# Gated delta rule in a fused two-block kernel: per-token norm factors in place of normalised keys and queries, and split gate rows spread in one pass

## What is computed

```
q = l2norm(q) * 128**-0.5 ; k = l2norm(k)          # per token and key head
g = -exp(a_log) * softplus(a + dt_bias) ; gc = cumsum(g)   # per chunk and value head
decay[i, j] = exp(gc[i] - gc[j]) for i >= j, else 0
L = strict_lower((k * beta) k^T * decay)
u, w = solve(I + L, [v * beta, k * beta * exp(gc)])
o = (q * exp(gc)) S + (q k^T * decay)(u - w S)      # S: the state of the chunk before
o = o * rsqrt(mean(o*o) + 1e-6) * norm_w * silu(z)
```

## Time and profile before

| what | before |
|---|---|
| median of 3 runs | 2850.68 us (2849.74 to 2850.77) |
| profiled execution: span, first to last instruction | 2847.0 us |
| PE, PEld, DVE, ACT, POOL busy | 96%, 84%, 68%, 42%, 29% |
| mean granted PE clock | 0.986 |
| the 8 iterations of the delta rule | about 170 to 975 us |
| one steady iteration | 98.86 us |

### The profile page before, as it was taken

How to read it: one execution, slowest core, us unless ns; L and a number is a source line. 1 busy time by engine, 2 the same in 40 slices (tenths; PEclk the granted TensorE clock), 3 DMA queues, 4 the chain that set the end, 5 groups by cost and what they waited for, 6 DMA issues and landing times.

```text
span 2847.0 us, 51314 instructions
## 1 busy us (share of the span) xinstructions
PE 2720.7 (96%) x20214; PEld 2404.2 (84%) x20214; DVE 1949.3 (68%) x2285; ACT 1208.2 (42%) x1521; POOL 812.5 (29%) x554
## 2 busy tenths in 40 slices
PE   6999999999997999999999999969999999999998
PEld 4788988898895777888888888769899999999996
DVE  1377877787778677666666666676999898555554
ACT  2255455545544444333333333344333334433343
POOL 1066666666667510000000000001555552000000
PEclk8999999999999999999999999989999999999999
DMA  9866666676665666666665555535554555555554
GB/s 364 311 195 214 223 216 200 205 247 199 200 223 169 212 184 207 187 191 189 188 188 187 189 189 186 167 115 169 156 171 148 157 169 172 179 185 183 184 201 147
DMA packets 283920, 552.72 MB, mean 194 GB/s; under 512 B 16817, under 2 KB 54258, under 8 KB 282610
## 3 DMA queue, kind: packets, MB, share of 16 engines
q1 hardware_dynamic: 263632, 474.02, 52.7%
q0 software_dynamic: 19408, 76.06, 7.2%
q10 hardware_dynamic: 722, 0.28, 0.0%
HBM read 548.19 MB, written 2.10 MB: 193 GB/s over the span
## 4 chain that ended last, share of the span: by engine, by line
PE 79%; DVE 11%; ACT 4%; issue 2%; DMA 2%; POOL 1%; DVEq 0%; SPq 0%; ACTq 0%; POOLq 0%; PEld 0%
PE pg L1130 20%; PE pg L1117 14%; PE pg L821 13%; PE pd L1130 11%; PE pd L1117 7%; PE pg L812 4%; DVE wl L2059 2%; PE pd L736 2%; DMA arena<-in_mod_w 1%; DVE arena L2340 1%; PE pd L985 1%; DVE arena L2342 1%; PE pd L1003 1%; DVE arena L2335 1%; PE pg L842 1%
## 5 line engine op out<-in xcount | busy, mean ns | idle before, releaser
L2059 DVE TENSOR_TENSOR wl<-wr,wh 128x1024 fp32r<-128x1024 f32 x616 | 773.0, 1264 | 515.7 <-ACT wh L1582 512.5
L1582 ACT ACTIVATE wh<-wr 128x1024 fp32r<-128x1024 f32 x616 | 652.6, 1060 | 1004.8 <-PE pg L1117 344.6
L595 POOL TENSOR_TENSOR wl<-wr,wh 128x1024 fp32r<-128x1024 f32 x195 | 479.8, 2462 | 394.3 <-ACT wh L1391 394.1
L1117 PE MATMUL pg<-hh,wh 128*128 128x256 f32 x1536 | 438.4, 285 | 3.9 <-ACT arena L1700 2.5
L1117 PE MATMUL pg<-hl,wh 128*128 128x256 f32 x1536 | 434.6, 283 | 0.0
L1117 PE MATMUL pg<-hh,wl 128*128 128x256 f32 x1536 | 434.3, 283 | 0.0
L1391 ACT ACTIVATE wh<-wr 128x1024 fp32r<-128x1024 f32 x216 | 227.7, 1057 | 349.3 <-PE pg L821 219.9
L821 PE MATMUL pg<-hh,wh 128*128 128x256 f32 x1024 | 301.2, 294 | 14.8 <-ACT arena L1439 12.0
L1117 PEld LDWEIGHTS pg<-hh,wh 128*128 128x128 f32 x1536 | 294.4, 192 | 16.6 <-issue 13.6
L1820 DVE SCALAR_TENSOR_TENSOR arena<-arena,condt 128x512 f32<-128x512 f32 x240 | 282.4, 1177 | 32.4 <-DMA arena<-in_mod_w 26.9
L1117 PEld LDWEIGHTS pg<-hl,wh 128*128 128x128 f32 x1536 | 294.5, 192 | 0.0
(11 more groups left out here) (392 smaller groups left out, 5323.6 us busy)
## 6 DMA issues: line engine op xcount, KB each, us to landing
wr<-in_w_in SPq DMA_DIRECT2D x224, 512.0 KB, 3.9
wr<-in_ffn_w_gu SPq DMA_DIRECT2D x176, 512.0 KB, 4.4
wr<-in_gdn_w_in SPq DMA_DIRECT2D x128, 512.0 KB, 4.3
arena<-in_mod_w POOLq DMA_DIRECT2D x64, 1024.0 KB, 7.7
wr<-in_ffn_w_down SPq DMA_DIRECT2D x88, 512.0 KB, 3.6
arena<-in_mod_w SPq DMA_DIRECT2D x32, 1024.0 KB, 12.2
wr<-in_gdn_w_in SPq DMA_DIRECT2D x128, 256.0 KB, 2.9
wr<-in_gdn_w_out SPq DMA_DIRECT2D x56, 512.0 KB, 4.6
```

Of the source, the lines that this page charges most:

```text
L595: nc.gpsimd.tensor_tensor(wl[c % RING][:], wraw[c % 4], wh[c % RING][:].bitcast(F32), ALU.subtract)\
L1117: m = nc.tensor.matmul(bank[:, n * T:(n + 1) * T], w[s][:, k, n * P:(n + 1) * P], act[x][:, k0 + k, :], skip_group_check=True, start=(firs ...
L1582: a(wh[c % 4][:], wraw[c % 4], ACT.Copy).then_inc(s_hc, 1)
L2059: v.tensor_tensor(wl[c % 4][:], wraw[c % 4], wh[c % 4][:].bitcast(F32), ALU.subtract).then_inc(s_lc, 1)
```

## The change

q and k stay as they are. The sums of squares are taken with 32 columns of ones into four partition groups (256 columns each), copied by ACT, transposed by PE to one value per token, and made into norms `sk` and inverse squares `rk2` per token on ACT; DVE puts `rk2` of k into the token factors of L (rows 2 and 3 of `tkc`), ACT puts the norm of k into v when it copies v. The norm of q is put into the constant under the last root: DVE adds `epsq` to the sums of squares of the output before ACT takes the logarithm. The gates are split into a high and a low part in 128 partitions (`gcs`), `rowm` has 128 partitions and type fp32r, and "rows" is one pass over 64 rows for each chunk of tokens. The core of the diff:

```
@@ program order
-VO = order("scal", "qkn", "dt", "lt", "lm", "at", "tc", "uc", *[f"{a}{s}" for s in LEVELS for a in ("x", "t")],
-           "x64", "u64", "md0", "o0", "rhs1", "o1", "oz", "md1", "on", "og")
-AO = order("rn", "exp", "kg", "vtok", "z", *[f"u{s}" for s in LEVELS], "v0", "s", "qs", "v1", "qkv", "rstd")
+VO = order("scal", "dt", "lt", "lm", "at", "tc", "uc", *[f"{a}{s}" for s in LEVELS for a in ("x", "t")],
+           "x64", "u64", "md0", "o0", "rhs1", "o1", "oz", "se", "md1", "on", "og")
+AO = order("rn", "exp", "sc", "kg", "vtok", "z", *[f"u{s}" for s in LEVELS], "v0", "s", "qs", "v1", "qkv", "sq", "rstd")
@@ POOL, batch
-                rows = gcT[0:2 * NH, 0:P].unsqueeze(1).broadcast_to([2 * NH, VH, P])
-                pick = pick2[:, bass.ds(it * VH, VH)].unsqueeze(2).broadcast_to([2 * NH, VH, P])
-                nc.gpsimd.tensor_tensor(rowm[0:2 * NH], rows, pick, ALU.mult).then_inc(s_g, 1)
+                rows = gcs[:, 0:P].bitcast(F32).unsqueeze(1).broadcast_to([P, VH, P])
+                pick = pick2[:, bass.ds(it * VH, VH)].unsqueeze(2).broadcast_to([P, VH, P])
+                nc.gpsimd.tensor_tensor(rowm[:], rows, pick, ALU.mult).then_inc(s_g, 1)
...
-            pool.wait_ge(s_v0, V0["gc"])
+            pool.wait_ge(s_v0, V0["gr"])
@@ PE, delta
                 if it:
+                    pe.wait_ge(s_v, bv - len(VO) + VO["o1"])
+                for n in range(4):
+                    m = nc.tensor.matmul(pd[0][32 * n:32 * n + 32, 0:T], ones[:, 0:32], sqb[:, n * T:(n + 1) * T],
+                                         start=True, stop=True)
+                m.then_inc(s_pe, 1)
+                yield
+                Ac("rn")
+                pe.wait_ge(s_g, bg + GO["rowm"])
+                if it:
                     pe.wait_ge(s_v, bv - len(VO) + VO["md1"])
                 else:
                     pe.wait_ge(s_a0, A0["tok"])
-                for n in range(2):
-                    m = nc.tensor.matmul(pd[0][:, n * 512:(n + 1) * 512], ones[:], sqb[:, n * 512:(n + 1) * 512],
-                                         start=True, stop=True)
-                m.then_inc(s_pe, 1)
-                yield
-                Ac("rn")
-                pe.wait_ge(s_g, bg + GO["rowm"])
-                for n in range(2):
-                    r = slice(NH * n, NH * (n + 1))
-                    m = nc.tensor.matmul(pd[0][:, n * 512:(n + 1) * 512], ones[r, :],
+                for n in range(TT):
+                    r = slice(64 * n, 64 * n + 64)
+                    m = nc.tensor.matmul(pd[0][:, n * 512:(n + 1) * 512], ones[r, :].bitcast(F32R),
                                          rowm[r].rearrange("p a b -> p (a b)"), start=True, stop=True)
                 m.then_inc(s_pe, 1)
                 yield
-                V("qkn")
...
                 V("dt")
+                for c in range(TT):
+                    tr(pd[0][:, T + c * P:T + (c + 1) * P], ssb[:, c * P:(c + 1) * P])
@@ ACT, delta
                 PEw("ssq")
-                link(a(rnb, pd[0][:], ACT.Ln, bias=cst[:, 0:1]))
-                link(a(rnb[:, 0:512], rnb[:, 0:512], ACT.Exp, scale=-0.5, bias=cst[:, 2:3]))
-                a(rnb[:, 512:1024], rnb[:, 512:1024], ACT.Exp, scale=-0.5).then_inc(s_a, 1)
+                a(ssb, pd[0][:, 0:T], ACT.Copy).then_inc(s_a, 1)
                 yield
                 V("dt")
                 a(dTb.rearrange("p a b -> p (a b)"), dTb.rearrange("p a b -> p (a b)"), ACT.Exp).then_inc(s_a, 1)
-                yield
                 PEw("ktok")
+                link(a(lnk, pd[0][:, T:2 * T].rearrange("p (c n t) -> p c n t", c=TT, n=4)[:, :, :, 0], ACT.Ln,
+                       bias=cst[:, 0:1]))
+                a(sk, lnk, ACT.Exp, scale=0.5)
+                a(rk2, lnk, ACT.Exp, scale=-1.0).then_inc(s_a, 1)
+                yield
                 for h in range(VH):
                     a(kg0[:, h, :], pd[0][:, (h // 2) * P:(h // 2 + 1) * P], ACT.Copy, scale=tkc[:, 6, h:h + 1])
...
                 squares(VH)
-                link(a(rstd, ssq, ACT.Ln, scale=1.0 / P, bias=cst[:, 0:1]))
+                act.sem_inc(s_a, 1)
+                V("se")
+                link(a(rstd, ssq, ACT.Ln, scale=1.0 / P))
                 a(rstd, rstd, ACT.Exp, scale=-0.5).then_inc(s_a, 1)
@@ DVE, prologue
-            v.tensor_copy(gx[NH:2 * NH, 3, 0:P], gx[0:NH, 3, P:T])
             v.tensor_scalar(gx[0:NH, 0, 0:P], gx[0:NH, 3, 0:P], -1.0, gx[0:NH, 3, P - 1:P], ALU.mult, ALU.add)\
+                .then_inc(s_v0, 1)
+            link(v.tensor_copy(gcs[0:NH], gxv(3)))
+            v.tensor_tensor(gcs[NH:2 * NH, 0:P], gx[0:NH, 3, 0:P], gcs[0:NH, 0:P].bitcast(F32), ALU.subtract)
+            v.tensor_copy(gcs[2 * NH:3 * NH, 0:P], gcs[0:NH, P:T].bitcast(F32))
+            v.tensor_tensor(gcs[3 * NH:P, 0:P], gx[0:NH, 3, P:T], gcs[0:NH, P:T].bitcast(F32), ALU.subtract)\
                 .then_inc(s_v0, 1)
@@ DVE, delta
-                Ac("rn")
-                done(v.tensor_tensor(qk.rearrange("p a b -> p (a b)"), qk.rearrange("p a b -> p (a b)"), rnb, ALU.mult))
                 PEw("rows")
...
                 PEw("gram")
-                Ac("exp")
+                Ac("sc")
+                link(v.tensor_tensor(tkc[:, 2:4, :].rearrange("p c (a b) -> p c a b", a=2),
+                                     tkc[:, 2:4, :].rearrange("p c (a b) -> p c a b", a=2),
+                                     rk2[:, :, 2:4].unsqueeze(3).broadcast_to([P, TT, 2, 2]), ALU.mult))
+                stt(out=epsq, in0=sk[:, :, 0:2], scalar=P * P * EPS, in1=sk[:, :, 0:2], op0=ALU.mult, op1=ALU.mult)
...
                 done(v.tensor_tensor(oz, ob, zt, ALU.mult))
+                Ac("sq")
+                eighth = ssq.rearrange("p (c a b) -> p c a b", c=TT, a=2)
+                done(v.tensor_tensor(eighth, eighth, epsq.unsqueeze(3).broadcast_to([P, TT, 2, 2]), ALU.add))
                 PEw("md1")
                 mod_sum(it, 1)
```

More of the change, by code:

```diff
@@ L133, in build @@
         identc = masks[:, 5, 0:64]
-        pick2 = masks[0:2 * NH, 5, 64:64 + NH]
+        pick2 = masks[:, 5, 64:64 + NH]
         vc = sb("vc", [P, 640])
@@ L193, in build @@
         Sb = take(VH, P)
-        rowm = take(VH, P)
+        rowm_at = at[0]
+        take(VH, P)
         msum = take(8)
-        take(VH * P - 8)
+        lnk = take(TT, 4)
+        sk = take(TT, 4)
+        rk2 = take(TT, 4)
+        epsq = take(TT, 2)
+        take(VH * P - 36)
         tk = take(7, NH)
-        tkc = take(7, VH)
+        tkc = take(8, VH)[:, 0:7, :]
         cwc = take(4, 8)
@@ L206, in build @@
         wm = [arena[:, o:o + 2048].rearrange("p (k n) -> p k n", n=512) for o in mod_at] + mw
+        gx_at = at[0]
         gx = take(4, T)
@@ L214, in over @@
             return nc.alloc_sbuf_tensor_at(name, [P, *shape], F32R, offset=byte)
+        rowm = over("rowm", arena_at + 4 * rowm_at, VH, P)
+        gcs = over("gcs", arena_at + 4 * (gx_at + T), T)
         NWB = KD * 64 + 96
@@ L921, in delta @@
                 pe.wait_ge(s_g, bg + GO["rowm"])
-                for n in range(2):
-                    r = slice(NH * n, NH * (n + 1))
-                    m = nc.tensor.matmul(pd[0][:, n * 512:(n + 1) * 512], ones[r, :],
+                if it:
+                    pe.wait_ge(s_v, bv - len(VO) + VO["md1"])
+                else:
+                    pe.wait_ge(s_a0, A0["tok"])
+                for n in range(TT):
+                    r = slice(64 * n, 64 * n + 64)
+                    m = nc.tensor.matmul(pd[0][:, n * 512:(n + 1) * 512], ones[r, :].bitcast(F32R),
                                          rowm[r].rearrange("p a b -> p (a b)"), start=True, stop=True)
@@ L1470, in delta @@
                 a(dTb.rearrange("p a b -> p (a b)"), dTb.rearrange("p a b -> p (a b)"), ACT.Exp).then_inc(s_a, 1)
+                PEw("ktok")
+                link(a(lnk, pd[0][:, T:2 * T].rearrange("p (c n t) -> p c n t", c=TT, n=4)[:, :, :, 0], ACT.Ln,
+                       bias=cst[:, 0:1]))
+                a(sk, lnk, ACT.Exp, scale=0.5)
+                a(rk2, lnk, ACT.Exp, scale=-1.0).then_inc(s_a, 1)
                 yield
-                PEw("ktok")
                 for h in range(VH):
                     a(kg0[:, h, :], pd[0][:, (h // 2) * P:(h // 2 + 1) * P], ACT.Copy, scale=tkc[:, 6, h:h + 1])
-                a(vtok[:, 0:VH, :].rearrange("p a b -> p (a b)"), pd[0][:, 512:1024], ACT.Copy).then_inc(s_a, 1)
+                act.wait_ge(s_a, it * len(AO) + AO0 + AO["sc"])
+                for h in range(2):
+                    m = a(vtok[:, 2 * h:2 * h + 2, :].rearrange("p a b -> p (a b)"),
+                          pd[0][:, 512 + h * T:512 + (h + 1) * T], ACT.Copy, scale=sk[:, 0, 2 + h:3 + h])
+                m.then_inc(s_a, 1)
                 yield
                 V("tc")
-                a(vtok[:, VH:8, :].rearrange("p (a b) t -> p a (b t)", a=2),
-                  pd[0][:].rearrange("p (a c) -> p a c", a=2)[:, :, 256:512], ACT.Copy).then_inc(s_a, 1)
+                for h in range(2):
```

(3 more changed lines are left out.)

8 lines of the change are left out of this document (2 added, 6 removed).

## The result

The changed kernel takes **2871.7 us** (median of 4 runs, 2870.9 to 2875.4), the kernel before 2850.3 in the same series: ratio 1.0077, 95% interval 1.0065 to 1.0090. Slower, by 21 us. A second series of five runs of the same kernel, beside the later experiments, gave 2869.8 (ratio 1.0068, 1.0054 to 1.0082); I compare the experiments with that. The profiled execution took 2875.4, its span is 2873.5.

What follows compares the result with a forecast made beforehand. PE, busy for 96% of the span, was taken to bound the kernel. Terms of -10.5 + 7 + 14 + 6 - 4.5 = +12 us, added to the median of 2850.68, gave 2862.7, range 2838 to 2874.

Steps and rivals of the forecast that it cites:

- rival C: Before "ktok": copies of `taps` also caught by POOL's subtractions, PE waits 0.9 us for "dt" each iteration; 2869, chance 0.15.
- E: Rival at "ssq": the column groups do not run side by side, so "ssq" saves nothing; 2870, chance 0.05.
- PE's work: "ssq" saves 1.1 us, "rows" 0.6, "ktok" loses 0.2: net 1.5 saved per iteration, -10.5 for the first seven.
- The seam: Before chunk 0, "se" waits for POOL's subtraction and the logarithm starts 1.0 us late; seven seams, +7.
- The middle: From chunk 3, "lt", "lm" and "tc" come late behind POOL and PE waits 2.0 us per iteration; seven times, +14.
- the forecast case: Whole kernel: all main terms hold, +12 us in sum, 2862.7; chance 0.40.
- The prologue: Before the first iteration, three new gate instructions may each wait for POOL, `conv` ends at 176, PE idles; +6.
- The last iteration: Before "gram", the normalising product is gone and POOL's 5.28 us wait is won, less new DVE instructions: -4.5.
- a new instruction is caught in its stead: Last iteration: a new DVE instruction waits behind POOL in place of the removed product, so the gain is 0.

Runs made afterwards that it cites:

- (2): Changed kernel with "lt" no longer waiting for "sc", the division of beta by k's squared norm left out: 2869.2 us, against 2869.8 for the changed kernel.
- (5): Changed kernel with sums of squares coming out of PE per token, Ln and both Exp right behind "ssq", no added transposes in "ktok": 2862.1 us.
- (3): Changed kernel with the four gate-splitting instructions moved down past the first squares and the second `conv` of the prologue: 2862.7 us.
- (9): Changed kernel where POOL, in the last iteration, waits for the end of each own subtraction before issuing the next: 2864.6 us.
- (11): Kernel before with two edits, POOL waiting for each own subtraction in the last iteration and ACT emptying z ahead of the logarithm: 2848.7 against 2850.3 us.
- (6): Changed kernel with POOL's five low parts of the output in the last iteration at steps 1, 3, 5, 7, 9 instead of 1 to 5: 2866.5 us.
- (8): Changed kernel with ACT emptying the z projection ahead of its wait for "se": 2863.8 us.
- (1): Changed kernel without "se", so the constant of the output's norm leaves out the norm of q: 2861.7 us.
- (7): Kernel before with the gate part alone (split gates, `rowm` over 128 partitions, "rows" in two fp32r passes): 2858.3 us.

## Why the prediction was right, and where it was not

2862.7 was forecast, 2869.8 to 2871.7 measured: slower, inside the range of 2838 to 2874, for mostly the reasons given. By the number alone it could as well be rival C (2869) or E (2870); the traces rule out E ("ssq" takes 0.64 us and not 1.72) and show C's mechanism in part. That the sum came out within 7 to 9 us has some luck in it, as the terms show.

- **PE's work**: forecast -1.5 for each iteration, measured -1.1 by the windows. "ssq" and "rows" are at 0.64 and 0.50 in the timeline (forecast 0.6 and 0.45, in the chain 0.57 and 0.42). The rest is in the steps next to them: by the chain of the iteration from 472.7 the eight transposes behind "ssq" take 1.04 instead of 0.87, "ktok" takes 1.10 behind its wait where it took 0.89 in an iteration without one, and the step behind the wait for "tc" 1.15 instead of 1.08. These 0.45 us make up the difference: 1.15 + 0.64 - 0.23 - 0.45 is 1.1.
- **The seam**: forecast +1.0, measured +0.8 in each, by the mechanism named: "se" ended 0.02 after POOL's subtraction. Six of the seven show as the wait for z; in the seventh PE waits for the squares before "ssq", 3.2 us instead of 2.4. Removing "se" gave 8.1, of which the wait for z is 4.7.
- **The middle**: forecast +2.0 (1.2, 0.8 and 0.3 one after the other), measured +0.84: "lm" lasts 4.30 and "tc" is late as worked out, but DVE catches up behind it. Of the two reasons I gave, DVE's wait for "sc" and ACT's high part queued behind it, (2) shows that taking the first away alone gives nothing, and (5) that taking both away removes the wait; the second alone wasn't tried.
- **Rival C** ("dt" behind the taps) came true beside the forecast, not instead of it: 1.3 us in every other iteration, and in the others a stretch at half clock of the same price. That the clock pays as well stood in no term. This 1.3, which the forecast case had at nothing, has made good the middle's error: -1.1 + 0.8 + 0.84 + 1.3 is 1.8, forecast 1.5. That the two errors cancel is luck.
- **The prologue**: forecast +6; the first iteration is 6.3 to 7.1 longer (forecast -1.5 + 1.0 + 2.0 + 6 = 7.5), and (3) gave 7.1 back. `conv` near 176: 175.27.
- **The last iteration** is the step that failed: forecast -4.5, measured +1.4 to +2.0. "The product is gone", so its wait is won: but the cause was POOL's unbroken row, and the row took the next instruction instead, longer (21.9 us instead of 10.79). (9), which adds only gaps to the row, shows it. I did name the case "a new instruction is caught in its stead", at 0; it was an old one, and it cost more than nothing. The failed term is 6 us of the 7 to 9 by which the forecast was low.

The rule that the prediction weighed (the Trainium skill, SBUF - State Buffer, "Who interferes with whom": whichever issues first has the port) fails here more plainly: L1838 asked at 896.56, when the subtraction of 894.86 was running and that of 897.21 had not begun, and nine went ahead.

## What to carry to other kernels

Where two engines exclude each other, taking out the instruction that loses does not give its wait back: the next one in line loses instead, and what lets it in is a gap in the engine that wins. The gap has its price where that engine is itself nearly late: 4.5 us won in the last iteration of (9), 1.8 lost in that of (11), whose other edit is at the seams. When a wait is added in the middle of an in-order engine, look first at what it issues for others behind it: here ACT's high part came some 2 us later, and taking away only the wait on DVE, which looked like the cost, gave nothing back. A saving in PE's work that adds idle time at the same place can be paid back by its clock.

## What the runs showed that I had not expected

- A DVE instruction with operands in SBUF that asks while POOL runs two-input subtractions without a gap waited for 4 (before, L1933, 10.79 us), for 2 (taps, 4.92 us) and for 9 of them (21.9 us); a gap of 0.08 us let it in (9). DVE instructions issued right behind one that had just had the place waited for one subtraction only ((6): 2.78, 2.20, 2.26 us), and those subtractions lasted up to 2.79 instead of 2.38. Why the two cases differ wasn't tried.
- Stretches of 3.4 us at a granted clock of 0.5, 1.3 to 1.5 us dearer each, came in the steady iterations of most variants, nearly all right behind the seam's idle time of 2.0 to 2.8 us (one, of the first series, behind a wait of 2.1 us at 755), and in none of the kernel before with 2.0 us, (8) with 1.7 or (11) with 1.7 at most. Two variants with 2.0 had some ((1) and (7)). The length of that wait alone doesn't decide; what does stayed open.
- Eight fp32 products with a stationary operand of 128 x 128 and a single column took 1.8 us, twice a set of eight transposes (0.88).
